# A planner's cost of one step raised, a norm moved into its own projection, and the last stage's scratch moved, in a two-layer streaming encoder on one core

## The chip, the cores and the metric

One core of a Trainium2 chip runs the whole program. The metric is the device time of one execution in microseconds (us). All data are fp32. Below, "us" always means the time on the core, and a "turn" is one piece of the kernel's own order of work, explained further down.

## The reference

Two layers run over 1,024 prompt frames and 32 sample frames of width 1,024. Cut to what matters here:

```python
for l in range(DEPTH):                                   # 2 layers
    aq, ..., cgate = mixer_inputs(rmsnorm(xp, norm1[l]), w_in[l], ...)   # one projection
    oa = diff_attn_prompt(aq, ak, av, lam)               # mixer A: softmax attention, 6 heads
    ob = dsa_prompt(bq, iq, iw, bk, bv, ik)              # mixer B: top-256 keys by an index score
    sc, oc = hgrn2_prompt(cq, ck, cg, cv)                # mixer C: gated linear recurrence
    xp = xp + merge_heads(oa, ob, oc, ...) @ w_out
    h, fc = conv_ffn(rmsnorm(xp, norm2[l]), hist0, ffn_up[l], ...)       # d_ff = 2816
    xp = xp + h
return rmsnorm(xp, final_norm), caches and states
```

`dsa_prompt` ranks all keys of a query by an indexer's score and keeps the 256 largest; the sample frames go through the same code with cached keys.

## The kernel before

The frames are cut in two halves: half 0 has 512 prompt frames and the 32 sample frames (544 columns), half 1 the other 512. Activations lie transposed, features on the partitions. `xT` holds the residual stream x of both halves, `xn` the normed x of one half, 8 tiles of 128 features each. A dense product is cut in column groups of 272 (half 0) or 256 (half 1).

**Turns.** The dense work is a fixed list, `TURNS`, of 1,044 turns: `f` and `t` are groups of the input projection, `wo` of the output projection, `a` and `g` of the FFN's up projection, `dn` of the down projection. `nsq`, `nsr` and `nsc` make a norm: the mean of squares (a product with a constant matrix), the root and reciprocal into `inv`, and the scaling of x into `xn`. The stages follow in the order P00, P01, F00, P10, F01, P11, F10, F11, Y1 (P = projection, F = output projection and FFN; then layer and half). The constant weights come through a ring of four tiles, `wring`, loaded by the queue of SyncE (SP). A group ends in one of two PSUM banks and is copied out by ScalarE (ACT); the residual is added by GpSimd (POOL).

**Mixers.** The mixers' work is a list of steps of four kinds for each of the four (layer, half) pairs m = 0 to 3: X (the indexer and the picks), B (both attentions), C (the recurrence) and M (a last norm). Below, X0 means the X steps of pair 0, and so on. A pick (lines 1545 and 1546) takes the 8 largest scores of each row (`MAX8`) and strikes them out (`MATCH_REPLACE8`) on VectorE (DVE); 32 picks make 256 keys, and two picks are one step. A step's attention work goes from PE (scores, line 911 or 926) to DVE (maxima), to ACT (exponentials, line 1265), to DVE (combination, lines 1585 and 1592), to PE (transposes, line 953), to ACT (copies) and to PE (values, line 970).

**The planner.** `weave` lays the steps between the turns before the program is built. `turn_time` gives each turn an expected time and `step_times` each step; the planner spreads the steps so that both lists run out together. It works on five stretches of turns, and all engines follow the one order, `PLAN`, that comes out. The time that stands for a step of two picks over nk keys (k is nk / 1000) is

```python
            elif what == "pick":
                out.append((0, 0, min(BURST, ROUNDS[h][y] - BURST * z) * 2 * (1.04 * k + 0.15), 0))
```

**The norm of half 1 in layer 0.** x of half 1 needs nothing that the kernel computes, so `_project` makes its mean of squares early, in the projection of half 0 ahead of the section "c" (two `nsq` and two `nsr` turns, with eight squares by ACT before each, line 1108). The scaling follows at the start of P01.

**The last stage.** In F11, 20 of the 22 blocks of the up projection are made by seven products of half-size blocks in place of eight (`SEVEN`, `PRODUCTS`, turns of kind `s`). They need four sums of weight blocks for each n (S1 to S4, made by POOL, line 1770), four sums of blocks of `xn` (T1 to T4, once, DVE) and seven additions for each n (DVE). Before the change S2 to S4 lie in `kv`, doubled, T1 to T4 in `scr` and the parts of the result in `bias`: buffers of the mixers, which are done by then.

Of the kernel before, what the change touches and what calls it, by code (L numbers as in the profile page):

```python
# [10 lines left out]
P = 128  # L11
# [40 lines left out]
for _g, _p, _x in FT:  # L52
    if _x == 0:
# [22 lines left out]


# [4 lines left out]
SEVEN = {(1, 1): range(1, NF - 1)}  # L82
Product = namedtuple("Product", "name s t")
PRODUCTS = (Product("P1", "A11", "B11"), Product("P2", "A12", "B21"), Product("P6", "S2", "T2"), Product("P5", "S1", "T1"),
            Product("P7", "S3", "T3"), Product("P3", "S4", "B22"), Product("P4", "A22", "T4"))

S_ORDER, T_ORDER = ("S3", "S1", "S2", "S4"), ("T3", "T2", "T4", "T1")

PROJS = [(0, 0), (0, 1), (1, 0), (1, 1)]
# [102 lines left out]

BLOCKS = [(l, h, n) for l, h in PROJS if (l, h) in SEVEN for n in SEVEN[l, h]]
BLOCK_Q = {}
for _t in TURNS:
    if _t.kind == "s":
        BLOCK_Q[_t.q] = BLOCKS.index((_t.l, _t.h, _t.n))
FIRST_OF = {}
for _k in range(len(TURNS) - 1, -1, -1):
    if TURNS[_k].q >= 0:  # L200
        FIRST_OF[TURNS[_k].q] = _k
# [111 lines left out]
BURST = 2  # L313
# [47 lines left out]
def step_times(kind, m):  # L361

    h = m % 2
    if kind == "X":
        out = []
        for what, y, z in PICK_STEPS[h]:
# [3 lines left out]
            elif what == "pick":  # L370
                out.append((0, 0, min(BURST, ROUNDS[h][y] - BURST * z) * 2 * (1.04 * k + 0.15), 0))
# [115 lines left out]
def build(nc, io):  # L487
    ctx = ExitStack()
    with ctx:
# [12 lines left out]
        xT, xn = sb("xT", [P, KD, T]), sb("xn", [P, KD, WMAX])  # L502
# [4 lines left out]
        res = sb("res", [P, NRES, GMAX])  # L507
        utail, atail = sb("utail", [P, NF, 4]), sb("atail", [P, NF, 2])
# [7 lines left out]
        kv2 = kv[:].rearrange("p s c -> p (s c)")  # L516
# [3 lines left out]
        projT, projN = io["projT"], io["projN"]  # L520

# [12 lines left out]
        s_ws, s_xs, s_fix = sem("s_ws"), sem("s_xs"), sem("s_fix")  # L534
# [70 lines left out]


        def w_block(t, name):

            i = BLOCKS.index((t.l, t.h, t.n)) % 2
            if name in ("S2", "S3", "S4"):  # L610
                a = 1536 * i + 512 * int(name[1]) - 1024
                return kv2[:, a:a + 512]
            a = {"A11": 0, "A12": 512, "A21": 1024, "S1": 1024, "A22": 1536}[name]
# [1374 lines left out]
```

## Time and profile before

| | |
|---|---|
| median of 3 runs | 4004.64 us (4002.97 to 4010.16) |
| the profiled execution | 4004.88 us |
| its span, first to last instruction | 4003.0 us |
| PE busy | 3717.8 us, 93% of the span |
| DVE, ACT, POOL busy | 2334.5, 1125.3, 758.4 us |
| mean granted TensorE clock | 0.964 |

The span is what the rows below measure; 1.9 us of the execution lie around it. The times in a row are from the span's start. A busy time of PE contains matmuls at half clock, so the mean clock is to be read beside it.

### The profile page before, as it was taken

To read this page: it belongs to the slowest core of one execution; us is meant where nothing else is said; L and a number is where in the kernel's file an instruction comes from. 1 tells how busy PE (TensorE), PEld (TensorE's weight loads), DVE (VectorE), ACT (ScalarE), POOL (GpSimd) and SP (SyncE) were. 2 spreads that over 40 slices of the span, in tenths; PEclk is the share of its full clock that TensorE was granted. 3 is DMA by queue.
4 is the path that set the end of the run, shared out by engine and by line. 5 is a ranking of instruction groups with operands and counts; after the bars stand their busy time and mean duration, and the time that the engine had idled before them with its cause. 6 is when DMAs were issued, how large, how long until landed. Compare 5 with 4: busy or idle time off the path is not lost. (4 is left out here: it accounts for less than half of the span.)

```text
span 4003.0 us, 54393 instructions
## 1 busy us (share of the span) xinstructions
PE 3717.8 (93%) x21676; PEld 2953.6 (74%) x21676; DVE 2334.5 (58%) x4713; ACT 1125.3 (28%) x2668; POOL 758.4 (19%) x812
## 2 busy tenths in 40 slices
PE   7978899999999999999899989999899999899998
PEld 5755678777877777777667877787767777688887
DVE  1663556599964553549546454289955655544542
ACT  1123333211134442321334233111134443312221
POOL 2200121201001032221000014313010001353344
PEclk9988899999999999999999999999999999899999
DMA  4322233412222132342221213333221122242223
GB/s 141 96 76 75 81 98 89 129 67 70 79 67 68 51 96 93 90 124 89 62 91 54 80 59 96 115 110 122 70 69 52 42 75 69 70 149 83 65 89 96
DMA packets 152757, 339.54 MB, mean 85 GB/s; under 512 B 30312, under 2 KB 70824, under 8 KB 139192
## 3 DMA queue, kind: packets, MB, share of 16 engines
q1 hardware_dynamic: 92728, 291.04, 23.3%
q10 hardware_dynamic: 59776, 45.02, 3.9%
q8 instruction: 172, 2.82, 0.3%
q14 instruction: 81, 0.66, 0.1%
HBM read 299.33 MB, written 36.68 MB: 84 GB/s over the span
## 5 line engine op out<-in xcount | busy, mean ns | idle before, releaser
L835 PE MATMUL PS<-xn,wring 128*128 128x272 f32 (+1 forms) x7168 | 1709.1, 398 | 73.1 <-ACT dense L1163 29.2
L835 PEld LDWEIGHTS PS<-xn,wring 128*128 128x128 f32 x7168 | 1387.1, 196 | 348.1 <-issue 48.7
L1776 POOL TENSOR_TENSOR xT<-xT,res 128x272 f32<-128x272 f32 (+1 forms) x320 | 252.6, 790 | 2391.9 <-ACT res L1118 2356.6
L835 PE MATMUL PS<-dense,wring 128*128 128x256 f32 (+1 forms) x2816 | 666.1, 395 | 17.8 <-DVE dense L1436 9.2
L835 PEld LDWEIGHTS PS<-dense,wring 128*128 128x128 f32 x2816 | 541.6, 195 | 118.4 <-issue 10.7
L1545 DVE MAX8 top<-scr 128x8 f32<-128x384 f32 (+6 forms) x418 | 367.4, 879 | 12.5
L1546 DVE MATCH_REPLACE8 scr<-top,scr 128x384 f32<-128x384 f32 (+6 forms) x418 | 359.8, 861 | 0.0
L1118 ACT ACTIVATE res<-PS 128x272 f32<-128x272 f32 (+1 forms) x320 | 123.9, 389 | 600.5 <-PE PS L835 576.4
L856 PE MATMUL PS<-wring,xn 128*128 128x256 f32 (+1 forms) x1152 | 266.0, 391 | 3.7 <-ACT dense L1132 3.7
L856 PEld LDWEIGHTS PS<-wring,xn 128*128 128x128 f32 (+1 forms) x1152 | 213.3, 187 | 50.0 <-ACT dense L1132 5.4
L835 PE MATMUL PS<-catT,wring 128*128 128x272 f32 (+1 forms) x1024 | 231.1, 387 | 2.5 <-DVE catT L1615 1.8
L835 PEld LDWEIGHTS PS<-catT,wring 128*128 128x128 f32 x1024 | 193.6, 190 | 39.7 <-issue 7.1
L953 PE MATMUL PS<-ident,scr 128*128 128x128 f32 (+1 forms) x902 | 153.3, 283 | 62.6 <-DVE scr L1585 22.7
L1126 ACT ACTIVATE dense<-PS 128x256 f32<-128x256 f32 (+1 forms) x176 | 68.1, 390 | 509.1 <-PE PS L835 472.6
L953 PEld LDWEIGHTS PS<-ident,scr 128*128 128x128 f32 (+1 forms) x902 | 97.7, 141 | 150.4 <-issue 64.8
L1574 DVE CUSTOM_DVE_ANT_0 scr<-PS,bias 128x128 f32<-128x128 f32 (+8 forms) x90 | 67.7, 752 | 233.4 <-PE PS L953 229.8
L1566 DVE TENSOR_REDUCE mx<-PS 128x1 f32<-128x128 f32 (+8 forms) x216 | 162.4, 752 | 37.3 <-PE PS L926 30.8
L1564 DVE MEMSET PS<- 64x64 f32 x192 | 21.5, 112 | 273.1 <-PE PS L926 272.6
L1805 POOL TENSOR_TENSOR dense<-dense 128x544 f32<-128x544 f32 (+3 forms) x28 | 36.8, 1315 | 729.4 <-ACT dense L1126 687.6
L1265 ACT ACTIVATE scr<-PS,ngm 128x128 f32<-128x128 f32 (+8 forms) x216 | 158.2, 735 | 56.3 <-DVE ngm L1567 55.0
L1161 ACT ACTIVATE dense<-PS 128x272 f32<-128x272 f32 (+1 forms) x136 | 53.2, 392 | 338.6 <-PE PS L835 338.5
L970 PE MATMUL PS<-scr,kv 128*64 128x128 f32 (+2 forms) x984 | 130.0, 278 | 11.6 <-ACT turned L1277 10.8
(196 smaller groups left out, 4127.5 us busy)
## 6 DMA issues: line engine op xcount, KB each, us to landing
wring<-in_wu SPq DMA_DIRECT2D x88, 1024.0 KB, 4.8
wring<-in_wf SPq DMA_DIRECT2D x88, 512.0 KB, 3.8
wring<-in_wo SPq DMA_DIRECT2D x64, 512.0 KB, 3.7
wring<-in_wd SPq DMA_DIRECT2D x96, 320.0 KB, 2.9
wring<-in_wd SPq DMA_DIRECT2D x64, 384.0 KB, 3.1
wring<-in_wn SPq DMA_DIRECT2D x16, 1024.0 KB, 5.4
kv<-out_projT ACTq DMA_DIRECT2D x48, 256.0 KB, 4.1
out_projT<-dense SPq DMA_DIRECT2D x40, 272.0 KB
```

What stands on the lines that cost most here:

```text
L835: mm = nc.tensor.matmul(PS[:, dbank(t.g0), 0:cw], wtile(t.q, i), rhs, start=(kk == a), stop=(kk == b - 1))
L856: mm = nc.tensor.matmul(PS[:u.w, dbank(t.g0), 0:CW], xn[:, kk, u.col:u.col + u.w], wtile(t.q, kk, CW), start=(kk == 0), stop=(kk == KD - 1))
L953: tr = nc.tensor.transpose(PS[:kw, bank, (kt % 4) * P:(kt % 4) * P + u.w], soft(s, 0)[:u.w, kt * P:kt * P + kw], ident[:u.w, :u.w])
L970: mm = nc.tensor.matmul(PS[r0:r0 + D, bank, 0:u.w], v[:kw, u.vt + kt, D * it.hh:D * it.hh + D], pt_of(it)[:kw, kt, 0:u.w], start=(kt == 0) ...
L1118: nc.scalar.activation(res[:, i % NRES, 0:cw], PS[:, dbank(t.g0), 0:cw], ACT.Copy).then_inc(s_ea, 1)
L1126: nc.scalar.activation(ub[:, R % 2, x, c:c + cw], PS[:, dbank(t.g0), 0:cw], ACT.Copy).then_inc(s_ea, 1)
L1265: nc.scalar.activation(dst, src, ACT.Exp, bias=ngm[:u.w, s % 4, x:x + 1], scale=scale_a if g == "a" else 1.0, accum_out=sums[:u.w, s % 4, ...
L1545: step(nc.vector.max(top[:u.w, :], wk))
L1546: step(nc.vector.match_replace(wk, top[:u.w, :], wk, SENTINEL))
L1566: step(nc.vector.tensor_reduce(mx[:u.w, i, x:x + 1], sc, AX, ALU.max))
L1574: step(nc.vector.tensor_tensor_reduce(out=soft(s, 0)[:u.w, 0:u.nk], in0=sc, in1=bias[:u.w, u.bias:u.bias + u.nk], scale=scale_b, scalar=-3 ...
L1776: nc.gpsimd.tensor_tensor(x, x, res[:, i % NRES, 0:cw], ALU.add).then_inc(s_res, 1)
```

## The change

Four things are changed.

1. `step_times` counts a pick 1.3 times as long (2.6 where 2 stood). The products, their number and their operands stay; only the order of `PLAN` moves.
2. The norm of half 1 in layer 0 is no longer begun in P00. `_project` now makes it at the start of P01, and the norm of its second column group after that stage's first group.
3. `xT` is laid out half by half, and x is loaded whole: eight transfers of 128x544 and eight of 128x512, where there were sixteen of 128x272 and eight of 128x512.
4. In F11 the order of the seven products is changed (P7 ahead of P5). S3 lies in `inv`, S2 in a new buffer `wsum`, S4 and S1 over blocks of the weights; none is doubled. T2 to T4 and the parts lie in the half of `xT` that is not used any more, and T2 to T4 are made right behind the norm. The new sums of POOL are spread over the turns of a block instead of standing at its start. Branches for other stages (`ASIDE`, `BACK`, `ON_POOL`) are there but empty.

The diff, cut to its core:

```diff
-    if l == 0 and h == 0:
+    if l == 0:
         _norm(l, h, 0, 0, 1)
-    elif l == 0:
-        _turn("nsc", l, h, 0, 1, 0, ng=0)
...
-        if (l, h, g) == (0, 0, "c"):
-
-            for j in range(2):
-                _root(0, 1, 0, j, 1)
         for n, j in order[2 * done:2 * end]:
             _turn("f", l, h, n, 0, j, load=("f", l, h, n, 0))
-            if (n, j) == (0, 0) and (l, h) == (0, 1):
-                _turn("nsc", l, h, 0, 1, 1, ng=0)
-            elif (n, j) == (0, 0):
+            if (n, j) == (0, 0):
                 _norm(l, h, 0, 1, 1 - l)
...
-                out.append((0, 0, min(BURST, ROUNDS[h][y] - BURST * z) * 2 * (1.04 * k + 0.15), 0))
+                out.append((0, 0, min(BURST, ROUNDS[h][y] - BURST * z) * 2.6 * (1.04 * k + 0.15), 0))
...
-        xT, xn = sb("xT", [P, KD, T]), sb("xn", [P, KD, WMAX])
+        xT, xn = sb("xT", [P, KD * T]), sb("xn", [P, KD, WMAX])
...
-                sp.eng.dma_start(xT[:, k, 0:GMAX], io["xT"][k * P:(k + 1) * P, 0:GMAX]).then_inc(s_x[0][k], 16)
+                sp.eng.dma_start(x_of[0][:, k, :], io["xT"][k * P:(k + 1) * P, 0:W[0]]).then_inc(s_x[0][k], 16)
...
-                    if nextq == 0:
-                        for kk in range(KD):
-                            sp.eng.dma_start(xT[:, kk, GMAX:W[0]], io["xT"][kk * P:(kk + 1) * P, GMAX:W[0]]).then_inc(s_x[0][kk], 16)
...
+            def weight_sum(B, name, x, y, op):
+
+                t = TURNS[LAST[("s",) + BLOCKS[B] + (0,)]]
+                i = 4 * B + S_ORDER.index(name)
+                pool.wait_ge(s_ws, i)
+                nc.gpsimd.tensor_tensor(w_block(t, name), w_block(t, x), w_block(t, y), op).then_inc(s_ws, 1)
+
+            def first_sums(B):
+
+                k = LAST[("s",) + BLOCKS[B] + (0,)]
+                weights_in(pool, TURNS[k].q)
+                pool.wait_ge(s_xn, KD * (norm_of(k) + 1))
+                if B:
+                    pool.wait_ge(s_mm, group_of(B - 1, "P7") + 1)
+                weight_sum(B, "S3", "A11", "A21", ALU.subtract)
+                weight_sum(B, "S2", "A22", "S3", ALU.subtract)
...
+                    if name == "P2":
+                        pool.wait_ge(s_mm, t.g0 + 1)
+                        weight_sum(BLOCK_Q[t.q], "S4", "A12", "S2", ALU.subtract)
+                    elif name == "P7" and next_block is not None:
+                        first_sums(next_block)
+                    elif name == "P3" and next_block is not None:
+                        weight_sum(next_block, "S1", "A21", "A22", ALU.add)
```

How the order moves is seen at three places. The first is PE's program in the picks of half 0 in layer 0 (X0). `PS<-scr` are the indexer's products, one set for each part of the scores that DVE then picks from; `PS<-xn,wring` and `PS<-wring,xn` are the dense groups of 8 matmuls; `PS<-heads,mean` is the mean of squares of half 1. Before:

```order
L875 MATMUL PS<-scr 128x512 x2
L835 MATMUL PS<-xn,wring 128x272 x40
L875 MATMUL PS<-scr 128x512 x2
L835 MATMUL PS<-xn,wring 128x272 x40
L875 MATMUL PS<-scr 32x512 x2
L875 MATMUL PS<-scr 32x32 x2
L835 MATMUL PS<-xn,wring 128x272 x16
L856 MATMUL PS<-wring,xn 128x256 x32
L856 MATMUL PS<-wring,xn 32x256 x8
L875 MATMUL PS<-scr 32x512 x2
L875 MATMUL PS<-scr 32x32 x2
L812 MATMUL PS<-heads,mean 128x256 x16
```

And now, from the same set of the indexer's products on:

```order
L941 MATMUL PS<-scr 128x512 x2
L901 MATMUL PS<-xn,wring 128x272 x56
L941 MATMUL PS<-scr 128x512 x2
L901 MATMUL PS<-xn,wring 128x272 x40
L941 MATMUL PS<-scr 32x512 x2
L941 MATMUL PS<-scr 32x32 x2
L922 MATMUL PS<-wring,xn 128x256 x32
L922 MATMUL PS<-wring,xn 32x256 x8
L901 MATMUL PS<-xn,wring 128x272 x32
L941 MATMUL PS<-scr 32x512 x2
L941 MATMUL PS<-scr 32x32 x2
L901 MATMUL PS<-xn,wring 128x272 x56
```

The dense work between two sets of the indexer has grown from 5 to 7, from 5 to 5, and from 7 groups (with the small one) to 9, and the 16 matmuls of the mean of squares are gone from here.

The second place is ACT's program at the start of P01, where the norm of half 1 now stands. `heads<-xT` are the squares, `inv<-PS` the root, `scr,sums<-PS` the exponentials of the attention with which it is interleaved, `kv<-` the loads of the attention's next operands, which ACT issues. Now:

```order
L1174 ACTIVATE heads<-xT 128x256 x8
L1261 DMA kv<-out_projT 128x544
L1268 DMA kv<-out_projT 128x512
L1269 DMA kv<-out_projN 128x4x128
L1271 DMA kv<-in_ak 128x512
L1272 DMA kv<-out_projT 128x32
L1273 DMA kv<-in_av 128x4x128
L1274 DMA kv<-out_projN 32x128
L1350 ACTIVATE turned<-PS 128x128
L1338 ACTIVATE scr,sums<-PS,ngm 128x256 x2
L1179 ACT_TABLE_LOAD
L1179 ACTIVATE inv<-PS,epst 128x256
```

Before, the squares and the root stood in the picks, with no exponential near, so that no table had to be changed for them:

```order
L1218 ACTIVATE scr<-PS 32x544 x2
L1108 ACTIVATE heads<-xT 128x256 x8
L1113 ACTIVATE inv<-PS,epst 128x256
L1108 ACTIVATE heads<-xT 128x256 x8
L1113 ACTIVATE inv<-PS,epst 128x256
```

What moved is the whole chain from the squares to the root, from behind the indexer's `scr<-PS` to between the attention's exponentials; it has gained two changes of table for each of the two column groups.

The third place is SP's queue at the very start. Before:

```order
L702 DMA mean<-in_mean 128x128
L704 DMA xT<-in_xT 128x272 x8
L724 DMA wring<-in_wf 128x1024
L766 DMA xT<-in_xT 128x272 x8
L724 DMA wring<-in_wf 128x1024 x3
L709 DMA par<-in_params 128x304
```

Now:

```order
L747 DMA mean<-in_mean 128x128
L749 DMA xT<-in_xT 128x544 x8
L769 DMA wring<-in_wf 128x1024 x4
L754 DMA par<-in_params 128x304
L754 DMA fgain<-in_fgain 128x8
```

Eight issues are gone ahead of the small constants; the bytes are the same. The place of every phase in the list of turns, read from the two plans (a phase ends where the next begins), with the sum of `turn_time` of its turns in the planner's own units:

| phase | turns before | planned | turns now | planned |
|---|---|---|---|---|
| X0, X1, X2, X3 | 34, 113, 50, 96 | 108, 355, 154, 314 | 36, 125, 58, 111 | 122, 398, 177, 352 |
| B0, B1, B2, B3 | 34, 73, 54, 61 | 109, 210, 156, 186 | 35, 67, 52, 51 | 105, 188, 147, 166 |
| C0, C1, C2, C3 | 42, 55, 70, 58 | 137, 188, 193, 168 | 39, 49, 64, 53 | 128, 167, 179, 150 |

In X0 before and in B0 now, 8 units are the two `nsq` turns of the moved norm.

## Rows read from the trace of the kernel before

**Rows 1.** The page: the span, and each engine's busy time.

```profile
span 4003.0 us, 54393 instructions
PE 3717.8 (93%) x21676; PEld 2953.6 (74%) x21676; DVE 2334.5 (58%) x4713; ACT 1125.3 (28%) x2668; POOL 758.4 (19%) x812
```

**Rows 2.** Busy time by window: X0, B0, C0, X1, B1, X2, B2, X3, B3, C3, F11.

```profile
110.00:258.00 148.00, 127.38 (x542) 97.28 (x541) 115.49 (x249) 23.10 (x59) 25.23 (x19) 0.93 0.32 97
258.00:528.00 270.00, 224.05 (x1171) 156.84 (x1171) 133.65 (x443) 91.19 (x294) 23.83 (x18) 0.87 0.24 73
528.00:738.00 210.00, 197.40 (x1900) 163.94 (x1900) 111.28 (x204) 73.18 (x155) 32.09 (x24) 0.96 0.31 91
738.00:1132.00 394.00, 381.95 (x1653) 306.54 (x1653) 353.16 (x566) 67.06 (x156) 58.06 (x78) 1.00 0.29 92
1132.00:1487.00 355.00, 341.41 (x1976) 253.35 (x1973) 189.53 (x439) 155.86 (x333) 55.81 (x67) 0.98 0.21 62
...
1753.00:1930.00 177.00, 164.75 (x738) 137.75 (x736) 148.56 (x319) 29.30 (x65) 31.63 (x46) 0.97 0.36 113
1930.00:2205.00 275.00, 256.08 (x1454) 190.82 (x1453) 143.53 (x472) 104.06 (x328) 18.64 (x25) 0.97 0.21 64
...
2549.00:2922.00 373.00, 347.46 (x1509) 284.15 (x1509) 324.32 (x497) 54.28 (x125) 56.35 (x64) 0.97 0.32 98
2922.00:3263.00 341.00, 331.51 (x1937) 244.72 (x1936) 182.02 (x421) 148.18 (x321) 27.25 (x32) 0.98 0.20 64
3263.00:3499.00 236.00, 215.68 (x1854) 168.99 (x1852) 134.42 (x261) 83.59 (x174) 46.73 (x57) 0.94 0.22 62
3499.00:4003.00 504.00, 482.33 (x2218) 420.57 (x2218) 223.72 (x345) 106.54 (x259) 215.05 (x226) 0.99 0.31 97
```

The columns are the window, its length, busy time (and instructions) of PE, PEld, DVE, ACT and POOL, the granted clock, the DMA engines' share and GB/s.

**Rows 3.** The timeline in the picks of X0, with the idle time before.

```profile
225.69 0.61 ACT L1218 ACTIVATE scr<-PS 32x544 f32<-32x544 f32 x1 [11.34 <-DVE scr L1535]
227.63 6.28 PE L812 MATMUL PS<-heads,mean 128*128 128x256 f32 x16 [12.71 <-ACT heads L1108]
```

**Rows 4.** PE's timeline: other idle times that DVE or ACT ended.

```profile
266.84 0.47 PE L953 MATMUL PS<-ident,scr 128*128 128x128 f32 x1 [8.01 <-DVE scr L1585]
...
2782.26 17.92 PE L835 MATMUL PS<-xn,wring 128*128 128x272 f32 x69 [7.01 <-DVE xn L1454]
...
2931.34 1.11 PE L953 MATMUL PS<-ident,scr 128*128 128x128 f32 x4 [4.19 <-DVE scr L1585]
```

**Rows 5.** The timeline at the start: SP's issues, DVE's first wait.

```profile
5.44 4.13 SPq L766 DMA_DIRECT2D xT<-in_xT  x8
19.78 0.16 DVE L1854 TENSOR_TENSOR omlb<-clow 128x3 f32<-128x3 f32 x1 [18.91 <-DMA scr<-in_lam]
```

**Rows 6.** Busy time by window at the start (columns as in rows 2).

```profile
0.00:20.00 20.00, 0.00 (x0) 0.00 (x0) 0.25 (x3) 1.28 (x1) 0.20 (x4) 1.00 0.87 277
```

**Rows 7.** Busy time by window behind that stall (columns as in rows 2).

```profile
227.00:234.00 7.00, 6.28 (x16) 4.78 (x16) 1.13 (x2) 2.63 (x9) 0.00 (x0) 0.58 0.00 0
```

**Rows 8.** The timeline: pieces of the norm's chain, and P01's start.

```profile
242.61 1.75 DVE L1447 RECIPROCAL inv<-inv 128x256 f32<-128x256 f32 x1
258.49 1.28 ACT L1265 ACT_TABLE_LOAD   x1
414.30 5.12 PE L835 MATMUL PS<-xn,wring 128*128 128x256 f32 x16 [3.27 <-DVE xn L1454]
430.86 0.34 ACTq L1188 DMA_DIRECT2D kv<-out_projT  x1
433.83 1.38 ACTq L1201 DMA_DIRECT2D kv<-out_projN  x1
```

**Rows 9.** The timeline in F11: one of four weight sums, two of seven products.

```profile
3716.69 1.59 POOL L1770 TENSOR_TENSOR wring<-wring 128x512 f32<-128x512 f32 x1
3593.89 1.89 PE L848 MATMUL PS<-scr,wring 128*128 128x256 f32 x8
3595.62 1.89 PE L848 MATMUL PS<-scr,kv 128*128 128x256 f32 x8
```

More of the change, by code:

```diff
@@ L193, with group_of @@
 BLOCKS = [(l, h, n) for l, h in PROJS if (l, h) in SEVEN for n in SEVEN[l, h]]
-BLOCK_Q = {}
-for _t in TURNS:
+BLOCK_Q, FIRST_OF = {}, {}
+for _k, _t in enumerate(TURNS):
     if _t.kind == "s":
         BLOCK_Q[_t.q] = BLOCKS.index((_t.l, _t.h, _t.n))
[L198 to L201, printed above, removed]
+    if _t.q >= 0 and _t.q not in FIRST_OF:
+        FIRST_OF[_t.q] = _k
+ASIDE = [x for x in SEVEN if x in ((0, 1), (1, 0))]
+BACK = [x for x in SEVEN if x != (1, 1)]
+def group_of(block, name):
+    return TURNS[LAST[("s",) + BLOCKS[block] + ([x.name for x in PRODUCTS].index(name),)]].g0
 TILE_DONE = [max(t.g0 + t.ng for t in TURNS if t.q == q) for q in range(len(TILES))]
@@ L507, in build @@
         res = sb("res", [P, NRES, GMAX])
+        wsum = sb("wsum", [P, 4 * P])
         utail, atail = sb("utail", [P, NF, 4]), sb("atail", [P, NF, 2])
@@ L520, in build @@
         projT, projN = io["projT"], io["projN"]
+        x_all = [xT[:, KD * C0[h]:KD * (C0[h] + W[h])] for h in range(2)]
+        x_of = [x_all[h].rearrange("p (k t) -> p k t", k=KD) for h in range(2)]
         ub = work_d[:, 0:2176].rearrange("p (s x t) -> p s x t", s=2, x=2)
@@ L618, in x_block @@
             (c0, cw), (c1, _) = GRP[h]
-            if name in T_ORDER:
-                a = 4 * GMAX * (int(name[1]) - 1)
-                return scr[:, a:a + 4 * cw].rearrange("p (k t) -> p k t", k=4)
-            k, c = {"B11": (0, c0), "B12": (0, c1), "B21": (4, c0), "B22": (4, c1)}[name]
+            if name in ("T2", "T3", "T4") or name == "T1" and (l, h) == (1, 1):
+                a = 4 * cw * (int(name[1]) - 2)
+                flat = scr[:, 0:4 * cw] if name == "T1" else x_all[1 - h][:, a:a + 4 * cw]
+                return flat.rearrange("p (k t) -> p k t", k=4)
@@ L1097, in dense_scalar @@
             for k, t in enumerate(TURNS):
-                if pending is not None and k > UP_END[pending[0:3]] + (2 if t.kind == "s" else TURNS[UP_END[pending[0:3]]].kind == "s"):
+                if pending is not None and k >= tanh_turn(t, *pending[0:3]):
                     l, h, n, U = pending
@@ L1440, in dense_vector @@
             for k, t in enumerate(TURNS):
-                if pending is not None and (t.kind == "dn" or k >= UP_END[pending[0:3]] + (4 if t.kind == "s" else 2)):
+                if pending is not None and k >= product_turn(t, *pending[0:3]):
                     product()
@@ new lines, in dense_vector @@
+                if t.kind == "s" and t.p == 0 and t.n == SEVEN[t.l, t.h][0]:
+                    b = lambda name: x_block(t.l, t.h, name)
+                    if (t.l, t.h) == (1, 1):
+                        dve.wait_ge(s_ct, NPAIR * 4)
+                    else:
+                        dve.wait_ge(s_mm, t.g0)
+                    nc.vector.tensor_tensor(b("T1"), b("B12"), b("B11"), ALU.subtract).then_inc(s_xs, 1)
+                if t.kind == "s" and (t.l, t.h) not in ON_POOL:
+                    add_products(dve, nc.vector, t)
```

190 lines of the change are left out of this document (114 added, 76 removed).

## The prediction

> **What bounds the kernel now.** I read the page first: PE is busy 3717.8 of 4003.0 us, so 285 us of idle time are all that an order of work can win, besides the clock [rows 1]. Nothing here removes a matmul, so PE's busy time stays but for its clock, and the question is which waits go and which come. So I cut the span at the turns where the planner's phases begin and asked for busy times by window [rows 2]. The reader is to see two kinds. In the picks (X) DVE is nearly full: 353.2 of 394 us in X1, 324.3 of 373 in X3, 148.6 of 177 in X2. PE still waits there: 20.6 us in X0, 12.1 in X1, 12.3 in X2, 25.5 in X3. In the attention phases (B) no engine but PE is near full (DVE has 133.7 of 270 us in B0), yet PE waits 46.0 us in B0 and 18.9 in B2, against 13.6 in B1 and 9.5 in B3: there the ring PE, DVE, ACT, PE of each step is what PE waits for, and dense groups fill the gaps. F11 has 21.7 us of idle time, at its ends. Last I looked at single waits, for what ended them [rows 3, 4].
>
> The sum is made against the profiled execution, 4004.9 us; the median of three runs, 4004.6, is the same for this purpose. Differences under 0.2% (8 us) can hardly be told from none, by the spread of the three runs.
>
> **1. The start.** DVE's first constants end its 18.9 us wait at 19.8 us, and ACT's and PE's first work follows them. Eight x issues, 4.1 us on SP's queue, go from ahead of them [rows 5]. If SP's issuing were the limit, 4.1 us would be won. But the DMA engines are 87% busy over these 20 us at 277 GB/s [rows 6], and the bytes ahead of the constants are the same: then nothing. In between, with wider rows: -2 (0 to -4).
>
> **2. The mean of squares leaves X0.** PE stands 12.7 us before it, since ACT must first pass the indexer's `scr<-PS`, which itself stood 11.3 us for DVE, deep in picks [rows 3]. Behind the stall the clock is 0.58 over 7 us with PE busy 6.3 [rows 7]: 2.9 us more. A second, short stall lies before the second column group, of about 1 us (X0's 20.6 less the big one hold it). All this is gone with the two turns: -16.6. No less, unless another ACT operation of a dense group is caught in the same place: group copies stand there as well, and PSUM's two banks give PE two groups, about 7 us, before it stops. Lower bound of the gain: 8.
>
> **3. The same norm in P01.** Now all of it lies between groups that need it. First, PE comes to `nsq` while ACT has a step of the attention before the squares: 2.5 us (0 to 5). Then ACT issues seven loads, which took from 430.9 to 435.2 us, 4.3 us, before it comes to a copy, two exponentials, a change of table, 1.28, and the root; then follow the reciprocal, 1.75, and one scaling [rows 8]. With my estimates of 2 for copy, exponentials and root and 0.4 for the scaling this is 9.7 us; the mean's own matmuls cover the first 0.5, and PE has three short pieces of attention to do, some 2: 7.2 left. For the second group ACT has a change of table, a copy, exponentials and eight squares behind PE's group of 3.5 us (as long as two products [rows 9]) and PE again some attention: 2. Its scaling is covered by the two groups of the first columns between. Sum 11.7, of which 3.3 was waited at this place before [rows 8]; with 1 for the clock: +9 (3 to 18). What is queued behind ACT's wait for the mean is the attention's next exponential, so B0's ring turns later by as much, which is in this number once, since PE has nothing else then.
>
> **4. Picks are laid wider.** The picks now have 36, 125, 58 and 111 turns. In planner's units the dense cover grows by 43 in X1, 23 in X2 and 38 in X3; at the measured busy time per unit (348 for 314 in X3, so 1.1) that is 47, 25 and 42 us. DVE, 84% to 90% full there, gains only the convolutions and products of those groups, some 4 to 8 us, and comes to 328 of about 415 in X3, 361 of 441 in X1, 153 of 202 in X2: under 83% [rows 2]. So DVE no longer falls behind step by step, and what PE lost by that goes: in X3 the 25.5, with 7.0 before a scaling, and 4.2 at B3's first transposes [rows 2, 4]. Of X1 and X2 a part are first waits of a stage, which stay. In X0 cover grows too, but DVE's picks are there the whole of the phase, and B0 can't begin before they end: of its remaining 6.9 and of the 8.0 at B0's first transposes [rows 2, 4] I take under half. Credit: X3 22, X2 7, X1 6, X0 6, together 41 of 69. The clock adds: it is 0.97 over X3's 373 us, which is 11 us of PE's time, and 1.00 over X1, where as many single waits are short [rows 2]. I take 7: -48. Bounds: 22 from X3 alone, and 69 with 10 of clock, 79.
>
> The Trainium skill (TensorE: Matmul & The Clock Gate, Part 1) has it that the slow clock is the default and activity releases it, so that a wait costs more than itself. By that alone every one of the 41 us would bring clock time back, and X1's 6 with them. X1's row, 12.1 us idle at a clock of 1.00, does not bear that out for short waits, and X3's does for its long ones; the sum goes by the rows, and by the page it would be some 5 us lower.
>
> **5. B and C pay for it.** Without the moved norm's 8 units, B0 loses 12 units of cover, B1 22, B2 9, B3 20, and the C phases 9, 21, 14 and 18: 125. What a unit is worth is read by comparing phases of the same steps. B0 and B2 do the same 59 steps with 109 and 156 units. B0 has 38 us of idle time without the 8.0 above, B2 18.9; half of the clock's loss (0.13 of 270, 0.03 of 275) adds 18 and 4. So 47 units are worth 33 us, 0.7 each: B0 and B2 lose 21 units, 15 us. B1 and B3, with 210 and 186 units, wait 13.6 and 9.5: no price at all. C0 and C3 wait 12.6 and 20.3 with 137 and 168 units: none either [rows 2]. But B3 goes below anything measured, from 186 to 166. I take 0.2 for the 104 units of these six, +21. Sum: +36. Bounds: 0 (there is slack in all of them), and 0.7 for all, 88.
>
> **6. The last stage.** Its PE time is seven products of under 1.9 us for a block [rows 9], 482.3 of 504 us busy in all [rows 2], with no wait inside the blocks worth a term. So an order that waits less has nothing to win. A weight sum took 1.6 us at most. S4 now begins when P2 has ended and P3 needs it, with P6, P7 and P5 between, 5.2 us at 1.73 from one product's start to the next [rows 9]; S3 and S2, 3.2 us, have the five products from P7 to the next P6, 8.6 us. The parts are not doubled now, but their additions end two products earlier than the next write. T2 to T4 are now three operations ahead of the first block's convolution, which is awaited three turns later. 0, covered by these slacks; if POOL came 3.6 us late the cover would be gone, and each further us would cost 20.
>
> **Sum:** -2 -16.6 +9 -48 +36 = -21.6, so 4004.9 - 21.6 = 3983 us.
>
> **The rivals.**
> *What the picks win is given back (no change).* If the wider picks win only their lower bound, 22, and B and C cost 30, with the terms 1 to 3 at -9.6, the sum is -2: 4003 us, between 3997 and 4012. For it speaks that each of the planner's stretches holds a fixed amount of dense work, so that every turn given to X is taken from B and C; against it that B1 and B3 show no price. 0.20.
> *The attention's ring becomes the bound (slower).* B3 gets 51 turns for 48 steps. Its mechanism: a step's transposes wait for DVE's combination, and with a dense group less between them PE stands a whole group, 3.5 us at a time. If every unit costs 0.7, as between B2 and B0, term 5 is 88 and the sum +30: 4035 us. From a price of 0.46 a unit on (58 us for 125 units, against the 57.6 of terms 1 to 4) it decides, and the norm between the exponentials at its upper end, +18, helps it. B0's 46 us speak for it, B3's 9.5 against. 0.14.
> *The last stage stalls (no change).* POOL's sums have less lead than doubled ones. 5 us of delay in each block would be 1.4 past the slack, 28 us: 4011 us with the rest as forecast. 0.03, for POOL is busy 215 of 504 us there.
> *The wider picks do nothing, since PE's waits there are of the first step alone.* Then DVE is not the cause, terms 4 and 5 are both near zero, and only the norm's move is left: -10, 3995 us. It ends with the forecast's sign. 0.05.
>
> **How the numbers follow.** The forecast, -10 to -45, has 0.58; its own range is 3960 to 3995. The range for all is 3956 to 4013: from above the full credit of term 4 beside a half of term 5, to the rival without change; the slower ones beyond it have about 0.12, what lies below 0.06. Faster by over 0.2% has the forecast and the last rival, and a little is taken off for units read from two phases only: 0.62. Within 0.2% lie the no-change rival and the last stage's, 0.23, of which the tails take 0.02. Slower is the ring, 0.14, and 0.03 of tails: 0.17. That leaves 0.21 for the same.
>
> **What would show it.** In the profile after: the 12.7 us stall gone from X0, and one or two of 2 to 8 us at P01's start, with changes of table around a root; X3's waits on DVE mostly gone, its window longer by some 20 to 40 us with DVE under 85%; B0 and B3 shorter, with more idle time for each step; F11 as before, 482 us of PE. The prediction is wrong if B3's or C's idle time grows by more than 10 us each, if P01's norm costs over 20 us, or if the picks' idle time stays.

## The result

The changed kernel took 3941.61 us (median of four executions, 3931.35 to 3948.37) against 4007.4 for the kernel before beside it: a ratio of 0.9824 [0.98, 0.9848]. It is faster, and by three times the forecast; 3983 was too high and 3942 lies below the range. The profiled execution took 3931.35 us, 73.5 less than that of before, and was the fastest of the four. The head of its page:

```profile
span 3929.5 us, 54494 instructions
...
PE 3692.2 (94%) x21676; PEld 2935.9 (75%) x21676; DVE 2321.4 (59%) x4713; ACT 1128.6 (29%) x2672; POOL 758.1 (19%) x812
```

PE has the same 21676 matmuls and is busy 25.6 us less [rows 1]: that is clock, as the account below shows. Its idle time in the span fell from 285 to 237 us. The same phases as in [rows 2], by window, columns as there: X0, B0, C0, X1, B1, C1, then X2, B2, C2, X3, B3, C3, F11.

```profile
105.00:251.00 146.00, 139.29 (x608) 107.35 (x608) 118.70 (x259) 19.64 (x48) 25.43 (x19) 0.98 0.39 116
251.00:516.00 265.00, 214.72 (x1152) 150.21 (x1151) 136.16 (x433) 100.82 (x312) 30.92 (x24) 0.88 0.22 68
516.00:715.00 199.00, 182.90 (x1851) 151.96 (x1850) 106.80 (x202) 72.16 (x152) 23.51 (x18) 0.98 0.31 91
715.00:1145.00 430.00, 424.38 (x1848) 343.00 (x1850) 367.33 (x598) 74.06 (x175) 59.71 (x78) 1.00 0.28 88
1145.00:1479.00 334.00, 321.19 (x1888) 234.04 (x1884) 178.45 (x409) 151.37 (x322) 64.86 (x74) 0.98 0.23 70
1479.00:1716.00 237.00, 229.40 (x1944) 179.48 (x1944) 109.27 (x187) 72.77 (x149) 41.46 (x30) 0.96 0.30 90
...
1716.00:1905.00 189.00, 185.26 (x857) 157.06 (x856) 158.23 (x334) 34.08 (x76) 34.68 (x50) 1.00 0.35 112
1905.00:2171.00 266.00, 249.85 (x1418) 185.15 (x1417) 134.92 (x456) 101.39 (x324) 20.33 (x28) 0.96 0.23 74
2171.00:2413.00 242.00, 228.45 (x1998) 188.92 (x1996) 145.24 (x267) 85.70 (x181) 49.42 (x62) 0.96 0.25 77
...
2483.00:2878.00 395.00, 383.38 (x1686) 315.51 (x1686) 330.51 (x506) 61.13 (x141) 68.66 (x79) 0.98 0.34 105
2878.00:3205.00 327.00, 309.17 (x1810) 225.45 (x1810) 176.94 (x419) 143.60 (x311) 16.07 (x17) 0.98 0.17 54
3205.00:3430.00 225.00, 200.39 (x1810) 156.55 (x1808) 132.26 (x254) 82.58 (x169) 46.84 (x57) 0.95 0.22 64
3430.00:3929.00 499.00, 480.99 (x2218) 421.05 (x2218) 207.54 (x345) 105.13 (x259) 213.74 (x226) 0.99 0.31 98
```

The reader is to take window less PE's busy time, and hold it against [rows 2]. The picks: X0 20.6 to 6.7, X1 12.1 to 5.6, X2 12.3 to 3.7, X3 25.5 to 11.6, with DVE at 84% in X3 and 85% in X1. The attention hardly moves: B0 46.0 to 50.3, B1 13.6 to 12.8, B2 18.9 to 16.2, B3 9.5 to 17.8. C1 and C2, which [rows 2] leave out, were these in the kernel before:

```profile
1487.00:1753.00 266.00, 252.08 (x2047) 199.00 (x2046) 112.21 (x187) 76.08 (x157) 53.52 (x38) 0.97 0.31 92
2205.00:2485.00 280.00, 254.71 (x2115) 211.75 (x2112) 147.47 (x274) 90.52 (x191) 52.77 (x69) 0.95 0.25 78
```

C0 and C3 grew, 12.6 to 16.1 and 20.3 to 24.6, C1 and C2 fell, 13.9 to 7.6 and 25.3 to 13.6. The windows are cut at whole microseconds, and C2's is longer before than after. Where sums of phases are compared below, and said to be by exact ends, a phase goes from the first dense matmul of its first turn to that of the next phase (C, with the norm behind it, to that of the next stretch). So counted, X has 78.5 us of idle time before and 26.0 after, B 82.3 and 98.9, C 69.4 and 62.8; the 8.01 us before B0's first transposes [rows 4] stand in X before, and in B by the windows.

For the runs below I use one account, summed over a trace: the span is PE's work at full clock, plus its idle time, plus half of what PE was busy while the granted clock was 0.5. (Every record of the clock here is either 0.5 or 1.) The first was 3596 to 3602 us in every kernel here, so two numbers tell a trace. Before: idle 285, busy at half clock 236. After: 237 and 182. So of the 73.5 us 48 are idle time and 27 are clock, less 1 for work. A ratio is to the kernel before in the same batch, whose median was 4007.4 us beside the changed kernel, 4011.5 beside e1 to e4, 4012.8 beside e5 to e8 and 4013.9 beside e9 to e12; ratios, and not medians, compare kernels of different batches.

| kernel | median us | ratio to before | profiled | PE idle | busy at half clock |
|---|---|---|---|---|---|
| before | 4007.4 | 1 | 4004.9 | 285 | 236 |
| after | 3941.61 | 0.9824 [0.98, 0.9848] | 3931.35 | 237 | 182 |
| e1_pick_only | 3961.94 | 0.9882 [0.9868, 0.9897] | 3960.71 | 239 | 238 |
| e2_no_pick | 4004.41 | 0.9984 [0.9971, 0.9996] | 4010.32 | 277 | 266 |
| e6_early_no_pick | 4001.11 | 0.9973 [0.9962, 0.9984] | 4003.58 | 279 | 248 |
| e4_norm_early | 3953.9 | 0.9863 [0.9849, 0.9878] | 3954.48 | 236 | 230 |
| e10_norm_early_again | 3959.56 | 0.9871 [0.9849, 0.9893] | 3953.37 | 238 | 227 |
| e5_after_again | 3949.78 | 0.9849 [0.9831, 0.9867] | 3941.86 | 236 | 205 |
| e11_after_third | 3949.42 | 0.9838 [0.9812, 0.9864] | 3945.07 | 239 | 204 |
| e3_pick_wider | 3970.8 | 0.9911 [0.9894, 0.9927] | 3967.47 | 255 | 230 |
| e7_last_pair_wider | 3920.95 | 0.9781 [0.9766, 0.9795] | 3919.96 | 223 | 190 |
| e8_attention_wider | 3923.57 | 0.9788 [0.9771, 0.9804] | 3916.32 | 238 | 150 |
| e9_best_of_stretches | 3908.95 | 0.9742 [0.9723, 0.9761] | 3910.55 | 221 | 177 |
| e12_sums_after_scaling | 4014.56 (one) | | 4014.56 | 292 | 245 |

### The profile page after: what moved, and what is told of

It reads as the page before. It is cut to its first block and busy times, and to the rows that moved or that the text cites. A ratio compares the mean times of both kernels' runs of the same rounds, so it can differ in the third digit from the quotient of the medians.

```text
span 3929.5 us, 54494 instructions
## 1 busy us (share of the span) xinstructions
PE 3692.2 (94%) x21676; PEld 2935.9 (75%) x21676; DVE 2321.4 (59%) x4713; ACT 1128.6 (29%) x2672; POOL 758.1 (19%) x812
## 5 line engine op out<-in xcount | busy, mean ns | idle before, releaser
L901 PE MATMUL PS<-xn,wring 128*128 128x272 f32 (+1 forms) x7168 | 1682.0, 394 | 33.9 <-DVE xn L1527 11.7
L992 PE MATMUL PS<-kv 32*128 32x512 f32 (+5 forms) x672 | 135.3, 510 | 11.5 <-ACT scr L1338 10.4
```

What stands on the lines that cost most here:

```text
L901: mm = nc.tensor.matmul(PS[:, dbank(t.g0), 0:cw], wtile(t.q, i), rhs, start=(kk == a), stop=(kk == b - 1))
L992: mm = nc.tensor.matmul(PS[:u.w, abank(s, u, x) + a // 512, 0:b - a], q[r, u.col:u.col + u.w], k[r, u.key + a:u.key + b], start=True, stop ...
```

## The experiments

**1. The pick's factor alone, and all but the factor.** e1 is the kernel before with one number changed; e2 is the changed kernel with that number put back.

```diff
-  out.append((0, 0, min(BURST, ROUNDS[h][y] - BURST * z) * 2 * (1.04 * k + 0.15), 0))
+  out.append((0, 0, min(BURST, ROUNDS[h][y] - BURST * z) * 2.6 * (1.04 * k + 0.15), 0))
```

> The kernel before with the pick's cost alone changed, 2 to 2.6; norm, x loads and last stage as before. Theory A (the wider picks made the win, and the attention and recurrence phases pay almost nothing for the cover they lose): 3945 to 3960 us, with the idle time of the four X phases together under 35 us and of B and C within 10 us of before's. Rival B (the plan is worth only what was forecast, and the rest came from the norm's move and the last stage): 3975 to 3990 us.

> The changed kernel with the pick's cost back at 2. Theory A: 3985 to 4000 us, so that two thirds or more of the 66 us go; stage F01, which only the plan changes, is back at about 721 us from 694. Rival B: 3955 to 3970 us.

e1 has nearly all of the idle time won, 239 against 237, and two thirds of the time; it lies 2 us above theory A's range. e2, everything else, is within 0.2% of before, 4 us above theory A's range and far from rival B's. The two gains, 1.2% and 0.2%, add up to less than the 1.5 to 1.8% of the changed kernel; experiment 3 has the rest. In e1 the mean of squares is still in X0, and its stall is nearly gone:

```profile
209.28 3.69 PE L812 MATMUL PS<-heads,mean 128*128 128x256 f32 x16 [0.92 <-ACT heads L1108]
```

In e6 (below: narrow picks, norm early), the same:

```profile
227.69 6.21 PE L885 MATMUL PS<-heads,mean 128*128 128x256 f32 x16 [12.78 <-ACT heads L1181]
```

In e2, where the norm has left, the dense group at this time:

```profile
227.28 13.94 PE L901 MATMUL PS<-xn,wring 128*128 128x272 f32 x48 [5.05 <-ACT dense L1192]
```

The 12.71 us of [rows 3] are 0.92 in e1, though the squares did not move. In e2, where they did, PE stands 5.05 at the next dense group, since ACT's copy of it stands in the same place, and 9.3 us at such groups in all of X0. The stall belonged to the picks, not to the norm. The other long wait there, 8.01 us before B0's first transposes [rows 4], goes with either part of the change. In e1:

```profile
260.40 0.33 PE L953 MATMUL PS<-ident,scr 128*128 128x128 f32 x1 [1.22 <-DVE scr L1585]
```

In e2 (a second wait of 1.21 us follows, so 2.7 in all):

```profile
256.74 0.33 PE L1019 MATMUL PS<-ident,scr 128*128 128x128 f32 x1 [1.47 <-DVE scr L1644]
```

**2. The norm's place alone, at either width.** e4 is the changed kernel with the second half's mean of squares and root in the first projection's stretch as before; e6 is that with the narrow picks.

```diff
-    if l == 0:
+    if l == 0 and h == 0:
         _norm(l, h, 0, 0, 1)
+    elif l == 0:
+        _turn("nsc", l, h, 0, 1, 0, ng=0)
...
+        if (l, h, g) == (0, 0, "c"):
+            for j in range(2):
+                _root(0, 1, 0, j, 1)
...
-            if (n, j) == (0, 0):
+            if (n, j) == (0, 0) and (l, h) == (0, 1):
+                _turn("nsc", l, h, 0, 1, 1, ng=0)
+            elif (n, j) == (0, 0):
```

> The changed kernel with the norm of half 1 back in the projection of half 0, ahead of section c; pick's cost 2.6, x loaded whole, last stage as changed. Theory A: with wide picks ACT is not far behind, so the old stall of 12.7 us at the mean of squares is mostly gone by itself, and the move is worth 5 us or less either way: 3935 to 3947 us. Rival B (the move itself was worth what the stall cost): 3952 to 3962 us.

> The changed kernel with the pick's cost at 2 and the norm of half 1 back in the projection of half 0: x loaded whole and the last stage as changed are what is left of the change. 3998 to 4004 us: some 4.5 us less in F11, where the scaling of the second column group is no longer slowed by POOL's weight sums, and 0 to 3 us at the start. If the norm's move alone was worth something at narrow picks, this is slower than the kernel without the picks' change (0.9984 of before) by that; I expect 5 us at most.

At narrow picks the move is worth nothing: e2 against e6, X0's idle time falls from 21.0 to 12.6 and the wait at B0's first transposes from 8.0 to 2.7, but the rest of B0 rises from 39.0 to 48.3. Of the 4.4 us less idle time nothing is left in the medians (ratios 0.9984 and 0.9973, intervals that overlap); the two profiles have 18 us more at half clock with the norm moved, but e2's is of its slowest execution. At wide picks e4's idle time is that of the changed kernel, as theory A has it, yet its 3953.9 us lie in rival B's range. Rival B's reason, the stall, is not there: in e1, with the norm as early, it is 0.92 us.

**3. The changed kernel again, and e4 again beside it.** All three are kernels already shown; the question is what varies.

> The changed kernel once more, unchanged, for the noise. If all that differs between equal orders is the clock: within 12 us of 3942, and in each of the planner's five stretches PE's time at full speed and its idle time within 2 us of the first profile, with the rest of any difference in the time that PE is busy at half clock. If idle times differ as well by more than 5 us in a stretch, comparisons of single profiles by stretch carry nothing.

> The changed kernel with the second half's mean of squares and root back in the first projection's stretch (the same kernel as the run of that name before, now in one batch with the changed kernel). Theory A (at wide picks the norm's place is worth nothing, since the picks' slack covers it either way): the same time as the changed kernel beside it within 0.2%, 8 us, and idle time within 3 us of 243. Theory B (the move is worth the 7 to 10 us that it seemed to be between batches): slower than the changed kernel by 0.15 to 0.3% with separate intervals.

> The changed kernel itself once more, in the same batch. Its idle time should be 237 us within 3, as twice before. What varies is the time that TensorE spends busy at half clock, 181 and 203 us in the two profiles of it so far. If that is only variation, a third profile falls anywhere between 175 and 210 us and the time moves by half of the difference, with the median near 3940 to 3950.

Idle time is the same to 3 us in all six profiles with the factor 2.6 everywhere, e1's among them, 236 to 239; between the first two profiles of the changed kernel it agrees within 1 us in each of the five stretches, so single profiles can be compared by their idle time. Half-clock time is not the same: 182, 205 and 204 with the norm moved, 238 (e1), 230 and 227 with it early. In one batch e10 took 3959.56 us and e11 3949.42, with intervals that overlap; so that batch alone doesn't give theory B its separate intervals. Over all batches the ratios are 0.9863 and 0.9871 against 0.9824, 0.9849 and 0.9838; taken by single executions, 8 against 12, the means are 0.9861 and 0.9837, 10 us apart, 3.5 times the standard error. So theory B holds in size: with the move the kernel is about 10 us faster at wide picks, and since idle time is equal, all of it is clock. At narrow picks the sign was the other (248 us at half clock with the norm early, 266 with it moved), one profile each. Where it comes up is odd. The B3 phase, 2500 us later, by window (columns as in [rows 2]), first e1:

```profile
2893.00:3227.00 334.00, 316.20 (x1812) 230.23 (x1812) 176.98 (x419) 144.08 (x311) 16.05 (x17) 0.96 0.17 52
```

e10:

```profile
2891.00:3225.00 334.00, 316.21 (x1818) 230.46 (x1816) 177.29 (x420) 143.95 (x311) 16.05 (x17) 0.96 0.17 52
```

e11:

```profile
2887.00:3214.00 327.00, 309.20 (x1808) 225.48 (x1810) 176.81 (x419) 143.72 (x311) 16.05 (x17) 0.98 0.17 54
```

PE's rows from P01's middle on stand in the same order in e10 and e11, the idle time of B3 is 17.8 us in all three, and the same work takes 316.2 or 309.2 us busy. The stretch from P11 to F10 took 1032.1, 1032.1 and 1031.9 us in e1, e4 and e10, and 1020.4, 1022.2 and 1025.3 in the three profiles of the changed kernel. So the same order with the same short waits ran at different clocks, in kernels that differ in what came early; why, no run here settles. One more run warns against laying all of it to the norm: e7 (below) has the changed kernel's order up to P11, and was busy at half clock 99 us in its first stretch, as the kernels with the norm early were (98 to 101), where the three profiles of the changed kernel had 67, 92 and 85.

**4. Wider still.** e3 takes 3.3 for every pick, e7 only in the last pair.

```diff
-  ... * 2.6 * (1.04 * k + 0.15), 0))
+  ... * (2.6, 2.6, 2.6, 3.3)[m] * (1.04 * k + 0.15), 0))
```

> The changed kernel with the pick's cost at 3.3, so that X gets 41, 139, 68 and 121 turns. The X phases have hardly any idle time left to give (26 us). Theory A (cover taken from B and C costs almost nothing): within 10 us of the changed kernel. Rival C (there is a price of 0.2 to 0.7 us for each unit of cover, and it was hidden by what X won): B and C lose another 9 to 20 units each, 120 in all, so 20 to 60 us slower, with the idle time in B and C.

> The changed kernel with the pick's cost at 3.3 for the last pair (m = 3) alone. If the 18 us that this stretch (P11 and F10) gained at 3.3 are real and the other stretches are independent of it: 3920 to 3933 us, with about 11 us less idle time in P11 and F10. If that was the clock alone: 3935 to 3948 us, with idle time as in the changed kernel.

e3 is slower than the changed kernel, as rival C has it, e7 faster, at the low end of its first range and with 12 us less idle time in P11 and F10. Cover is the dense work laid between the steps of a phase, in the planner's units. In e3 the price stands in B1 and B2, whose cover fell to 168 and 137 units: idle 21.8 and 24.0 us, from 12.8 and 16.2, and in C2 (22.8, from 13.2). X1 had nothing left to win (3.4). The last pair still had: X3, B3 and C3 of e7.

```profile
2490.00:2913.00 423.00, 416.11 (x1847) 343.88 (x1845) 338.35 (x526) 66.83 (x154) 69.38 (x80) 1.00 0.34 105
2913.00:3222.00 309.00, 292.63 (x1766) 212.53 (x1767) 177.06 (x418) 141.75 (x307) 16.34 (x16) 0.99 0.15 48
3222.00:3420.00 198.00, 177.04 (x1693) 137.37 (x1691) 127.65 (x236) 79.49 (x159) 47.81 (x58) 0.95 0.25 71
```

X3's idle time went from 11.6 to 6.9 at a clock of 1.00, and B3, 18 units poorer, waits 16.4 us, not 17.8. DVE is at 80%.

**5. Cover given back to the attention.** e8 lets ACT's and DVE's share of B's groups count 1.3 times in the planner, beside the wide picks. B has then 719 units against 607 after and 661 before.

```diff
-  out.append((3.5 * k + 0.2, 0.5 + 2.1 * k, 0.6 + 2 * k, 0))
+  out.append((3.5 * k + 0.2, 1.3 * (0.5 + 2.1 * k), 1.3 * (0.6 + 2 * k), 0))
...
-  out.append((5 * k + 0.3, 0.9 + 3.2 * k, 1.3 + 4.6 * k, 0))
+  out.append((5 * k + 0.3, 1.3 * (0.9 + 3.2 * k), 1.3 * (1.3 + 4.6 * k), 0))
```

> The changed kernel with the attention's steps (B) counted 1.3 times as long: B gets 19, 37, 27 and 31 units of cover more, X loses 7, 25, 13 and 20, C 12, 8, 14 and 11. The forecast's price of 0.7 us for a unit in B0 and B2: their idle time (50 and 16 us) falls by 13 and by all 16 us. Rival (cover has no price in B, its idle time comes from single waits that stay): B's idle time together within 8 us of 97, and X and C lose a little: 3945 to 3970 us.

B's idle time fell by 24 us (99 to 75 by exact ends), 6 us each in B0 and B2: less than one theory and more than the other had. X and C took it back (26 to 43, 63 to 71), so the total is 238 us as after. Still the kernel is 26 us faster than the changed kernel beside it, and 18 than its first median: half-clock time is 150 us. B0, B2, X3 and B3 by window:

```profile
243.00:523.00 280.00, 235.27 (x1296) 167.79 (x1295) 139.75 (x443) 104.16 (x325) 31.20 (x24) 0.91 0.23 73
...
1895.00:2175.00 280.00, 270.08 (x1548) 204.34 (x1547) 141.88 (x470) 105.57 (x334) 23.36 (x32) 0.99 0.25 77
2480.00:2864.00 384.00, 363.01 (x1587) 297.06 (x1587) 331.88 (x506) 57.05 (x132) 62.33 (x71) 0.98 0.33 99
2864.00:3211.00 347.00, 339.09 (x1991) 252.92 (x1990) 182.93 (x431) 149.58 (x326) 22.08 (x25) 1.00 0.20 62
```

The clock rose in B0 (0.88 to 0.91), B2 (0.96 to 0.99) and B3 (0.98 to 1.00), and X3 with 21 us of idle time stays at 0.98. Against the mean of the changed kernel's three profiles, B has 24 us less idle time and 42 us less at half clock (52 for 94), X 18 us more idle time and 2 us more at half clock (22 for 20). So the waits taken out of B had cost clock, and those added to X cost little; not nothing, for X has 16 to 22 us at half clock in all these profiles. That B's waits stand between the short matmuls of steps and X's between long runs of dense groups fits this, but it was not varied by itself.

**6. The best of each stretch.** e9 takes the factors (2.6, 2.6, 2.6, 3.3) and the 1.3 for B in the first pair alone, so that each stretch is that of the kernel in which it was shortest.

> The changed kernel with two edits to the plan's costs: a pick counts 2.6 in the first three pairs and 3.3 in the last, and VectorE's and ScalarE's share of B's groups counts 1.3 times as long in the first pair alone. Each stretch between two projections is then the one of the kernel that was shortest there so far. Theory A (each stretch's length is set by its own order alone): the sum of the shortest stretches, 711 + 1000 + 691 + 1002 + 498 us, so 3905 us, idle time of TensorE near 226 us, and at least 15 us under the two kernels that have one of the edits (3920.95 and 3923.57). Theory B (what one stretch gains, the next pays, or the shortest were lucky draws of the clock): 3920 or more, with the idle time at 226 all the same if it was the clock.

The stretches came out at 715, 999, 692, 1003 and 499 us, for 711, 1000, 691, 1002 and 498, and the median at 3908.95: theory A, within 4 us. Its third sign came out close: 12.0 and 14.6 us under the two kernels by medians, 16 and 18 by ratios, where at least 15 was forecast. What is gained in one stretch is not given back in the next. It is the fastest version here, 0.9742 [0.9723, 0.9761].

**7. The last stage.** F11 and what follows took 503.9 us in before and e1, and 498.3 to 499.4 in each kernel with the new last stage. Its idle time fell from 20.2 to 17.0 us, and what went is the wait for the scaling of the second column group. Before, what PE waited for in F11 (us in total, times, longest; the changed kernel has no such wait):

```profile
PE PS L835 <- DVE xn L1454: 3.2, 5, 0.7
```

Before, in the timeline (GpSimd's weight sums, the eight scalings, the groups that wait for them):

```profile
3563.14 1.27 POOL L1770 TENSOR_TENSOR kv<-wring 128x512 f32<-128x512 f32 x1
3563.92 8.59 DVE L1454 SCALAR_TENSOR_TENSOR xn<-xT,par,inv 128x256 f32<-128x256 f32 x8
...
3567.56 0.70 PE L835 MATMUL PS<-xn,wring 128*128 128x256 f32 x2 [0.70 <-DVE xn L1454]
```

After:

```profile
3494.94 3.26 DVE L1527 SCALAR_TENSOR_TENSOR xn<-xT,par,inv 128x256 f32<-128x256 f32 x8
...
3498.34 2.27 POOL L1823 TENSOR_TENSOR inv<-wring 128x512 f32<-128x512 f32 x1 [6.83 <-DVE xn L1527]
```

Eight scalings took 8.59 us beside the sums and 3.26 without. The sums wait now because S3 is written over `inv`. e12 gives the kernel before only that wait:

```diff
+                    pool.wait_ge(s_xn, KD * (norm_of(FIRST_OF[z.q]) + 1))
                     for i, (out, x, y, op) in enumerate((("S3", "A11", "A21", ALU.subtract), ...
```

> The kernel before with one wait more: in the last stage GpSimd starts on the sums of weights only when the scaling of the second column group is done (which the changed kernel has as a side effect of its scratch lying in a part of x). Theory A (the two engines stand in each other's way while both read and write SBUF): the eight scalings take 3.3 us in sum instead of 8.6, the stalls of TensorE at them go, and the last stage is 4 to 5 us shorter (499.4 instead of 503.9). Theory B (the gain came from the scratch's place or another part of the new last stage): the scalings stay at 8 to 9 us and the stage at 504.

Its timeline:

```profile
3571.49 3.26 DVE L1454 SCALAR_TENSOR_TENSOR xn<-xT,par,inv 128x256 f32<-128x256 f32 x8
...
3582.41 2.28 DVE L1462 TENSOR_TENSOR scr<-xn 128x1024 f32<-128x1024 f32 x1
...
3583.69 2.13 POOL L1771 TENSOR_TENSOR kv<-wring 128x512 f32<-128x512 f32 x1
...
3587.00 3.75 PE L848 MATMUL PS<-scr,kv 128*128 128x256 f32 x8 [3.71 <-issue]
```

The scaling is cured, as theory A has it, but the stage is not shorter: it took 506.0 us, in the one execution that there is. The sums now lie beside DVE's sums of x for the products, both slow down (1.22 to 2.28, 1.27 to 2.13), and PE waits 3.71 us before a product. The row names no releaser; DVE's second sum for the products ended 0.1 us earlier. The rest is half-clock time (6.6 us for 1.2). The changed kernel has the same crowding, 2.2 us each, but there the x sums stand ahead of the first block's convolution and P7 follows P6, so nothing waits. That the order is what saves it is read from the rows; it was not changed by itself.

The Trainium skill (SBUF — State Buffer, Who interferes with whom) says that a VectorE instruction with two SBUF inputs contends with a GpSimd one that reads SBUF, and of VectorE's two-port modes that whoever issues first has the shared ports for the whole instruction while the other is fully blocked. These rows agree on the pair. On who pays they show two cases: the scalings took 8.59 us for 3.26 while the weight sums stayed at 1.27 to 1.33, and in e12 both sides were slower.

## Why the prediction was wrong

Its direction and the mechanism of the picks held. Its size failed at term 5, the price of cover taken from B and C, and at the clock: of the forecast -21.6 us idle time was -18.7 and clock -2.9, and the two profiles have -48 and -27. The range failed with them. Its lower end, 3956, does not follow from the text's own bounds: term 4 in full, 79, beside half of term 5, 18, gives 3934.

**Term 1, the start (-2): right.** PE's idle time up to X0 fell from 29.4 to 26.9 us. SP's rows and DVE's first wait, for [rows 5]:

```profile
11.57 4.22 SPq L757 DMA_DIRECT2D xT<-in_xT  x8
...
17.34 0.16 DVE L1937 TENSOR_TENSOR omlb<-clow 128x3 f32<-128x3 f32 x1 [16.47 <-DMA scr<-in_lam]
```

**Term 2, the norm leaves X0 (-16.6): wrong as a cause.** Alone, at narrow picks, it was worth 8.4 us of X0 (e2 against e6), the lower bound that the text named with its reason: a copy caught in the same place. It also took 5.3 us from B0's first transposes, which no term had. With wide picks there is no stall to remove. The kernel got its 12.7 us, but the wider picks alone do it (e1).

**Term 3, the norm in P01 (+9): too high in this kernel.** At wide picks B0 paid 3.2 us (48.6 in e10, 51.8 in e11, by exact ends); at narrow ones it paid 9.3 beside the first transposes (e6 against e2), just the forecast. PE's rows there in the changed kernel, the two means, the transposes between and the first group:

```profile
347.24 5.36 PE L878 MATMUL PS<-heads,mean 128*128 128x256 f32 x16 [1.89 <-ACT heads L1174]
...
356.06 0.44 PE L1019 MATMUL PS<-ident,scr 128*128 128x128 f32 x2 [1.72 <-DVE scr L1651]
...
359.67 5.96 PE L901 MATMUL PS<-xn,wring 128*128 128x256 f32 x16 [2.80 <-DVE xn L1527]
...
369.50 3.69 PE L878 MATMUL PS<-heads,mean 128*128 128x256 f32 x16 [2.65 <-ACT heads L1174]
```

For ACT's step 2.5 was forecast and 1.89 waited, for the second mean 2 and 2.65. The seven loads stood among the squares and beside the mean's matmuls, not between mean and root. So from the mean's end to the first group it was 7.1 us and not 9.7, of which PE waited 1.72 and 2.80, 4.5 for the 7.2 of the text.

**Term 4, the picks (idle -41): right in size.** Together with term 2's 13.7 us of idle time it promised 55; X lost 44.5 (70.4 to 25.9 by exact ends, without the first transposes) and B0's first transposes another 6.8 (8.01 [rows 4] to the 1.22 of the row below). X3 won 13.9, not 22, and X1 and X2 17, not 13.

```profile
257.28 0.33 PE L1019 MATMUL PS<-ident,scr 128*128 128x128 f32 x1 [1.22 <-DVE scr L1644]
```

**Term 5, B and C pay (+36): this step failed.** The same phases with different cover show it (by exact ends, the first transposes counted to B): idle time of B against units is 75 at 719 (e8), 90 at 661 (before), 99 at 607 (after), 113 at 550 (e3): 38 us for 169 units, some 0.23 each. C has 71, 69, 63 and 68 us at 580, 687, 624 and 566 units: no steady price, and single places move it (C2 has 22.6 us in e8, 23.5 before, 13.2 after, 22.8 in e3). So the change cost 54 units x 0.23 = 12 us in B and none in C. e1, with the norm early, gives the same directly: without the first transposes B went from 82 to 96 us. Measured for B and C together is 160 to 162. The 0.7 came from B0 against B2, which differ in more than cover: B0 still waits 44.7 us in e8, with 124 units. The clock in it was also read too low: PE was busy at half clock 59.9 us in B0 and 14.2 in B2 before, which costs 30 and 7 us and not the text's 18 and 4, and would have made the price 0.9. A difference between two phases does not say what a unit is worth in one of them. What PE waited for in B3 (us in total, times, longest), before:

```profile
PE PS L953 <- DVE scr L1585: 4.7, 2, 4.2
PE PS L953 <- DVE scr L1592: 3.0, 4, 0.9
```

After:

```profile
PE PS L1019 <- DVE scr L1644: 13.2, 7, 2.2
PE PS L1019 <- DVE scr L1651: 4.3, 5, 1.3
```

That is the slower rival's mechanism, seven stops for DVE's combination instead of two, but of 2.2 us at most where it had a whole group of 3.5 at each. B3's 8.3 us stayed under the 10 from which the text called itself wrong, and C3's 4.3 too.

**The clock: this failed too.** Terms 2 to 4 had -9 in it, and 14 of the 33 us from which term 5 took its 0.7 were clock, +6 for its 21 units; the two profiles differ by -27. Over the four kernels with narrow picks half-clock time was 236, 266, 248 and 245 us, mean 249; with wide picks and an early norm 238, 230 and 227, mean 232; with the norm moved 182, 205 and 204, mean 197. Halved, that is 8 us with the wide picks and 17 more with the moved norm, at wide picks. The first is near the 7 of term 4; the second had no term, and why it came is open (experiment 3). Part of the 27 is luck of the profile: the first profile of the changed kernel had the least half-clock time of three, 11 us of time under the other two.

The Trainium skill (TensorE: Matmul & The Clock Gate, Part 1) has the throttled state as the default and activity as what releases it, and says that the chip's watch on activity runs free of the program, so that one kernel starts with more or fewer slow matmuls from run to run. The 182, 205 and 204 us at equal idle time agree with the second, and over the whole span, not the start alone. On the first, the weighing in the prediction took idle time as one sort, and e8 shows that it isn't: 238 us of it went with 150 us at half clock there and with 238 in e1.

**Term 6, the last stage (0): missed 4.5 us.** It looked for waits inside the blocks and for late sums, and not at what two engines do to each other at the scaling ahead of them.

Sum of what the runs showed: start -2.5, X -44.5, B and C +2, last stage -3.2 of idle time, clock -27 and work +1: the -73.5 between the two profiles, rounded. With the mean of the changed kernel's three profiles, 197 us at half clock, the clock is -19 and the sum -66, as between the medians.

## What to carry to other kernels

A planner's cost for an engine is tried out best by stretch: raise it in one stretch, read that stretch's idle time, and combine the best, since here the stretches added up to within 4 us. The price of cover taken from a phase is read from the same phase with other cover, not from another phase that waits more. And sort idle time before counting it: here that between the attention's steps cost clock as well, and that in the picks little. A stall beside an engine that is nearly full may be that engine's and not the instruction's that stands there: the 12.7 us at the mean became 5.05 at the next group when the mean was taken away, and 0.92 when the picks were spread.

## What the runs showed of the hardware

B3 with the same order and 17.8 us of idle time ran at a clock of 0.96 in e1 and e10 and 0.98 in the changed kernel and e11, 7 us in 327 (23 us busy at half clock in the first two, 9 in the others), and the kernels differ only in what came 2500 us earlier or, for e1, in the last stage, the start and the norm. The changed kernel's half-clock time differed by 23 us between profiles at idle times of 236 to 239. In e8 237.9 us of idle time went with 150 us busy at half clock, in e1 238.6 with 238.

Eight scalings of 128x256 with three inputs in SBUF took 3.26 us alone and 8.59 beside GpSimd's sums, while those sums stayed at 1.27 to 1.33; x sums of 128x1024 and weight sums of 128x512 beside each other went from 1.22 to 2.28 and from 1.27 to 2.13.
